# Banded attention: weights normalised inside their transposition, by diagonal tiles of reciprocals; squares of x moved to ScalarE, two merge gates computed earlier, and four changes of instruction order

## The reference, cut to what matters

```python
# start of block 1: modulated norms of x (512 tokens) and ctx (256 tokens)
h = rms_norm(x, g) * (1 + scale) + shift          # scale, shift = silu(c) @ w_mod
# each of the two layers of block 2
h = _rmsnorm(x, g_mix[l])
y_a = _mla(...)
y_b = _hgrn2(...)                                  # gates f = lb + (1-lb) * sigmoid(z), log f, scans
y_c = _window_gqa(c_q, c_k, c_v, rel_bias, c_sink[l])
merged = (jax.nn.sigmoid(gate_a) * (y_a @ w_br_a[l])
          + jax.nn.sigmoid(gate_b) * (y_b @ w_br_b[l])
          + jax.nn.sigmoid(gate_c) * (y_c @ w_br_c[l]))
x = x + merged @ w_out[l]
# _window_gqa: 8 heads of 64, blocks of 128 queries, each against 3 blocks of 128 keys
s = q @ k.T * 64 ** -0.5 + bias                    # bias: one relative-position line per head
m = maximum(max(s), sink)
p = exp(s - m)
p = p / (sum(p) + exp(sink - m))
o = p @ v
```

## Time and profile before

| | us |
|---|---|
| median of 3 runs (3956.91 to 3962.54) | 3962.54 |
| the profiled execution, its own time | 3960.44 |
| its span | 3958.6 |
| TensorE busy | 3691.1 (93%) |
| VectorE busy | 1956.9 (49%) |
| ScalarE busy | 1513.3 (38%) |
| GpSimd busy | 839.1 (21%) |
| mean granted TensorE clock | 0.959 |

### The profile page before, as it was taken

How to read it: one execution, slowest core, us unless ns; L and a number is a source line. 1 busy time by engine, 2 the same in 40 slices (tenths; PEclk the granted TensorE clock), 3 DMA queues, 4 the chain that set the end, 5 groups by cost and what they waited for, 6 DMA issues and landing times.

```text
span 3958.6 us, 60620 instructions
## 1 busy us (share of the span) xinstructions
PE 3691.1 (93%) x25506; PEld 3021.2 (76%) x25506; DVE 1956.9 (49%) x3020; ACT 1513.3 (38%) x2536; POOL 839.1 (21%) x832
## 2 busy tenths in 40 slices
PE   6989888999999989997999999998899799999998
PEld 3678877987888757786888788875677688878886
DVE  6656555535534565645333543437466533454343
ACT  4533223323323346644233422234565422343222
POOL 2222122221211123442110020202254311002120
PEclk7989998989999999998999999999999899999999
DMA  6310120013222202110223222220111022322222
GB/s 236 121 40 3 23 60 8 3 54 106 96 96 96 72 20 75 59 65 33 96 98 122 73 96 96 96 86 32 59 65 60 27 96 96 107 96 93 99 96 85
DMA packets 81111, 300.87 MB, mean 76 GB/s; under 512 B 8776, under 2 KB 9928, under 8 KB 79944
## 3 DMA queue, kind: packets, MB, share of 16 engines
q1 hardware_dynamic: 80840, 296.99, 22.0%
HBM read 292.76 MB, written 4.19 MB: 75 GB/s over the span
## 4 chain that ended last, share of the span: by engine, by line
PE 74%; DVE 11%; ACT 6%; issue 5%; POOL 3%; DMA 1%; SPq 0%; DVEq 0%; POOLq 0%; ACTq 0%
PE ps L208 72%; DVE wlo L239 2%; PE ps L213 1%; DVE he L247 1%; DMA wraw<-weights 1%; DVE ac L247 1%; ACT whi L227 1%; DVE hc L2419 1%; ACT ha L227 1%; DVE ha L239 1%; POOL p L243 1%; DVE ss L247 1%; ACT wp L228 1%; ACT L227 1%; DVE q L239 1%
## 5 line engine op out<-in xcount | busy, mean ns | idle before, releaser
L239 DVE TENSOR_TENSOR wlo<-wraw,whi 128x1024 fp32r<-128x1024 f32 x537 | 690.0, 1289 | 796.0 <-ACT whi L227 795.5
L208 PE MATMUL ps<-hh,whi 128*128 128x512 f32 x1840 | 728.7, 396 | 9.6 <-DVE hl L239 4.6
L208 PE MATMUL ps<-hl,whi 128*128 128x512 f32 x1840 | 720.5, 392 | 0.0
L208 PE MATMUL ps<-hh,wlo 128*128 128x512 f32 x1840 | 720.3, 391 | 0.0
L227 ACT ACTIVATE whi<-wraw 128x1024 fp32r<-128x1024 f32 x537 | 559.9, 1049 | 237.8 <-PE ps L208 187.1
L208 PEld LDWEIGHTS ps<-hh,whi 128*128 128x128 f32 x1840 | 347.8, 189 | 88.9 <-ACT hh L227 5.9
L208 PEld LDWEIGHTS ps<-hh,wlo 128*128 128x128 f32 x1840 | 348.0, 189 | 73.7
L208 PEld LDWEIGHTS ps<-hl,whi 128*128 128x128 f32 x1840 | 348.2, 189 | 70.5
L208 PE MATMUL ps<-u,u 64*64 64x64 f32 (+2 forms) x6016 | 229.2, 229 | 25.5 <-DVE u L239 16.8
L208 PEld LDWEIGHTS ps<-u,u 64*64 64x64 f32 (+1 forms) x6016 | 209.7, 140 | 42.8 <-DVE u L239 18.6
L208 PE MATMUL ps<-gh,whi 128*128 128x512 f32 x528 | 205.4, 389 | 0.0
(11 more groups left out here) (399 smaller groups left out, 7056.2 us busy)
## 6 DMA issues: line engine op xcount, KB each, us to landing
wraw<-weights SPq DMA_DIRECT2D x537, 512.0 KB, 3.2
x<-xT SPq DMA_DIRECT2D x2, 2048.0 KB, 9.8
bias_lines<-ln SPq DMA_DIRECT2D x1, 2048.0 KB
xmf<-memT SPq DMA_DIRECT2D x2, 1024.0 KB, 4.6
out<-x SPq DMA_DIRECT2D x1, 2048.0 KB, 6.2
bias<-bias_lines SPq DMA_DIRECT2D x1, 1536.0 KB, 8.7
con<-consts SPq DMA_DIRECT2D x1, 1379.0 KB, 16.6
ctxt<-ctxT SPq DMA_DIRECT2D x1, 1024.0 KB, 18.5
```

What stands on the lines that cost most here:

```text
L208: self.last, self.open = self.e.matmul(out, lhsT, rhs, start=start, stop=stop, skip_group_check=skip), True
L239: return self.e.tensor_tensor(out, a, b, op)
```

## The change

Seven edits, of which the first two belong to `window`.

1. VectorE makes only the reciprocals (`dve_inverse`). GpSimd writes, for each of the four row blocks, a 128x128 tile `dg` with the reciprocals on its diagonal, and TensorE turns the weights by an ordinary product with that tile, in place of a transposition by the identity. The multiplications of the weights on both engines go.
2. The gate projections of merge step 0 for the branches b and c are made in `window`: b ahead of the scores of step 1, c ahead of the turns of step 4. Gate b is copied to `stash`, later to `pre`, and its sigmoid stays in `merge`; gate c holds its PSUM bank.
3. All squares of x and ctx are made on ScalarE; GpSimd adds them in pairs (4 additions in place of 7), and TensorE sums four tiles in place of one: 16 products for x in place of 4, 8 for ctx in place of 2.
4. In the start, VectorE and ScalarE feed fewer weight blocks ahead before their next own step.
5. In `chunks` of half 0, VectorE feeds one block more before the bias add `dve_mod`.
6. The DMA of `bias_lines` is issued by ScalarE, not SP.
7. In `hgrn`, head 0, ScalarE takes the logarithms ahead of the values.

```diff
+            L.stash = self.sb("pre", W + 19968, [128, 512])
+            L.dg = self.ring(f"dg{l}", [self.sb("dg", W + 17920 + 128 * i, [128, 128]) for i in range(4)], lambda l=l: K.ended("hgrn", l))
+            L.pre = self.sb("pre", W + 33280, [128, 512])
...
+    def pool_pairs(self, tag, sq):
+        pool = self.pool
+        for k in range(0, 8, 2):
+            pool.wait_ge(self.act.at("sq", *tag, k + 1))
+            pool.tt(sq[k], sq[k], sq[k + 1], ALU.add).then_inc(pool("sq2", *tag, k // 2), 1)
...
-        K.pe_sums(lat, [K.HSQ[:, 0, :]], 4, lambda k: K.pool.at("acc", *lat))
+        K.pe_sums(lat, [K.HSQ[:, k, :] for k in range(0, 8, 2)], 4, lambda k: K.pool.at("sq2", *lat, k))
...
-        K.act_squares(lat, [K.HSQ[:, k, :] for k in ks8], [K.x[:, k, :] for k in ks8], K.loaded("x"))
+        K.act_all_squares(lat, [K.HSQ[:, k, :] for k in ks8], [K.x[:, k, :] for k in ks8], K.loaded("x"))
...
-        K.act_feed("mod", 1, ahead=2)
+        K.act_feed("mod", 1, ahead=0)
...
-        K.dve_feed("mod", 1, ahead=1)
+        K.dve_feed("mod", 1, ahead=0)
         K.dve_mod(0)
...
+            if (hg, kind, i, step) == (1, "q", 1, 0):
+                act.wait_ge(act.at("ln"))
+                act.e.dma_start(K.line, K.LN.unsqueeze(1).broadcast_to([8, 128, 512])).then_inc(K.s_load["lines"], 16)
...
-                K.dve_feed("c", *z)
                 new, old = K.mod_step(hg, c)
+                K.dve_feed("c", *z, ahead=1 if new is None else 2)
...
+    def dve_inverse(self, tag, n):
+        dve, act, sm = self.dve, self.act, self.sml[tag]
+        su, re = sm[:, 16:16 + n], sm[:, 24:24 + n]
+        dve.wait_ge(act.at("sink", *tag), act.at("p", *tag, n - 1))
+        dve.tt(su, su, re, ALU.add).then_inc(dve("su", *tag), 1)
+        dve.wait_ge(dve.at("su", *tag))
+        dve.e.reciprocal(re, su).then_inc(dve("re", *tag), 1)
+        dve.also("sml", *tag)
...
+                for dd in range(2):
+                    lns(i, dd)
                 if i == 0:
                     values()
-                for dd in range(2):
-                    lns(i, dd)
...
+            if c == 1:
+                K.pe_gate(l, 0, "b")
...
+            if c == 4:
+                K.pe_gate(l, 0, "c", hold=True)
...
-                        pe.wait_ge(K.divided(z, n))
+                        pe.wait_ge(K.pool.at("dg", *z, n), act.at("p", *z, n))
                         for j in range(k1 - k0):
-                            pe.tr(b[:, j * 128:j * 128 + 128], L.wP[z][:, n, j * 128:j * 128 + 128], K.con("id"))
+                            pe.mm(b[:, j * 128:j * 128 + 128], L.wP[z][:, n, j * 128:j * 128 + 128], L.dg[(*z, n)])
...
+                if (c, e) == (0, 1):
+                    act.wait_ge(pe.at("mg", l, 0, "b"), K.ended("hgrn", l))
+                    act.cp(L.stash, ps["mg", l, 0, "b"]).then_inc(act("stash", l), 1)
+                    act.also("ps", "mg", l, 0, "b")
...
+            if c == 2:
+                K.dve_feed("mg", l, 0, "b")
+            if c == 3:
+                K.dve_feed("mg", l, 0, "b", ahead=2)
...
-            K.pool_divide(z, [p[:, n, 0:w] for n, _, _, w, _ in K.spans()])
+            for n in range(4):
+                d = L.dg.take(pool, *z, n)
+                pool.wait_ge(K.dve.at("re", *z))
+                pool.tt(d, K.con("id"), K.sml[z][:, 24 + n:25 + n].broadcast_to([128, 128]), ALU.mult).then_inc(pool("dg", *z, n), 1)
...
+    def pe_gate(self, l, j, n, hold=False):
+        K = self
+        K.proj(("mg", l, j, n), K.win(l, "g" + n, j), [(K.ps.take(K.pe, "mg", l, j, n, hold=hold), K.h["mix", l])])
...
+                early = j == 0 and n == "b"
+                act.wait_ge(act.at("pre", l) if early else K.pe.at("mg", l, j, n))
+                act.a(g, L.pre if early else ps["mg", l, j, n], ACT.Sigmoid).then_inc(act("mg", l, j, n), 1)
...
-            if b == K.block_of["c", 1, "q", 1] + NRAW:
-                K.load("lines", K.line, K.LN.unsqueeze(1).broadcast_to([8, 128, 512]), act.at("ln"))
```

More of the change, by code:

```diff
@@ L735, in squared, with act_all_squares @@
         return (self.dve if k % 2 else self.act).at("sq", *tag, k)
+    def act_all_squares(self, tag, sq, xs, *ready):
+        act = self.act
+        for k in ks8:
+            act.wait_ge(*ready)
+            act.a(sq[k], xs[k], ACT.Square).then_inc(act("sq", *tag, k), 1)
+    def pool_pairs(self, tag, sq):
[3 more added lines that the diff above has]
+            pool.tt(sq[k], sq[k], sq[k + 1], ALU.add).then_inc(pool("sq2", *tag, k // 2), 1)
     def pe_sums(self, tag, sq, nt, ready):
@@ L894, in pe_start @@
         K.pe_mod(0, range(4, 8))
-        K.pe_sums(ctx, [K.CSQ[:, 0, :]], 2, lambda k: K.pool.at("acc", *ctx))
+        K.pe_sums(ctx, [K.CSQ[:, k, :] for k in range(0, 8, 2)], 2, lambda k: K.pool.at("sq2", *ctx, k))
         K.pe_mod(1, range(4))
@@ L912, in act_start @@
         K.act_feed("mod", 2)
-        K.act_squares(lat, [K.HSQ[:, k, :] for k in ks8], [K.x[:, k, :] for k in ks8], K.loaded("x"))
+        K.act_all_squares(lat, [K.HSQ[:, k, :] for k in ks8], [K.x[:, k, :] for k in ks8], K.loaded("x"))
         K.act_mod(2, K.mrow)
-        K.act_squares(ctx, [K.CSQ[:, k, :] for k in ks8], [K.CT[:, k, :] for k in ks8], K.loaded("ctx"))
+        K.act_all_squares(ctx, [K.CSQ[:, k, :] for k in ks8], [K.CT[:, k, :] for k in ks8], K.loaded("ctx"))
         K.act_mod(3, K.mrow)
         K.act_mod(0, K.mrow)
-        K.act_feed("mod", 1, ahead=2)
+        K.act_feed("mod", 1, ahead=0)
         K.act_shift(lat, range(4), K.x, K.HHI, 0)
@@ L940, in dve_start @@
         lat, ctx = ("lat",), ("ctx",)
-        K.dve_feed("mod", 2)
-        K.dve_squares(lat, [K.HSQ[:, k, :] for k in ks8], [K.x[:, k, :] for k in ks8], K.loaded("x"))
         K.dve_feed("mod", 2, ahead=2)
-        K.dve_squares(ctx, [K.CSQ[:, k, :] for k in ks8], [K.CT[:, k, :] for k in ks8], K.loaded("ctx"))
-        K.dve_feed("mod", 3, ahead=1)
+        K.dve_feed("mod", 3, ahead=0)
         K.dve_mod(2)
@@ L948, in dve_start @@
         K.dve_root(lat, 4, 1.0 / 1024)
-        K.dve_feed("mod", 0, ahead=1)
+        K.dve_feed("mod", 0, ahead=0)
         K.dve_mod(3)
@@ L970, in dve_scale @@
         for k in ks8:
-            dve.wait_ge(K.pe.at("rb", *tag), dve.at("gain", which), K.squared(tag, k))
+            dve.wait_ge(K.pe.at("rb", *tag), dve.at("gain", which), K.act.at("sq", *tag, k))
             dve.stt(v[:, k, :], v[:, k, :], K.gain[:, which, k:k + 1], ALU.mult, b[:, 0:T], ALU.mult).then_inc(dve("nv", *tag, k), 1)
@@ L985, in pool_start @@
         for tag, sq, nt in ((("lat",), K.HSQ, 4), (("ctx",), K.CSQ, 2)):
-            for k in range(1, 8):
-                pool.wait_ge(K.squared(tag, k - 1), K.squared(tag, k), pool.at("acc0", *tag, k - 1) if k > 1 else None)
-                pool.tt(sq[:, 0, :], sq[:, 0, :], sq[:, k, :], ALU.add).then_inc(pool("acc0", *tag, k), 1)
-            pool.also("acc", *tag)
-            if tag == ("lat",):
-                pool.wait_ge(K.loaded("consts"))
+            K.pool_pairs(tag, [sq[:, k, :] for k in ks8])
+            pool.wait_ge(K.loaded("consts"))
             K.pool_root(tag, nt)
@@ L2666, in act_window @@
         for c in range(5):
+            if c == 1:
+                K.act_feed("mg", l, 0, "b")
+            if c == 4:
+                act.wait_ge(act.at("stash", l), act.at("exped", l))
+                act.cp(L.pre, L.stash).then_inc(act("pre", l), 1)
+            if c == 3:
+                K.act_feed("mg", l, 0, "b", ahead=2)
             for i in (2 * c - 2, 2 * c - 1) if c > 0 else ():
@@ L2711, in dve_window @@
                     z = ("ws", l, 2 * c - 2 + e)
-                    K.dve_divide(z, [L.wP[z][:, n, 0:w] for n, _, _, w, _ in K.spans()], sink=True)
+                    K.dve_inverse(z, 4)
             for e in range(2) if c < 4 else ():
@@ L2796, in pe_merge @@
             for n in "abc":
-                bg, bb = ps.take(pe, "mg", l, j, n), ps.take(pe, "mb", l, j, n)
-                K.proj(("mg", l, j, n), K.win(l, "g" + n, j), [(bg, h)])
+                if j > 0 or n == "a":
+                    K.pe_gate(l, j, n)
+                bb = ps.take(pe, "mb", l, j, n)
                 cols = slice(j * 128, j * 128 + 128)
@@ L2817, in act_merge @@
                 g = L.mg.take(act, l, j, n)
-                act.wait_ge(K.pe.at("mg", l, j, n))
-                act.a(g, ps["mg", l, j, n], ACT.Sigmoid).then_inc(act("mg", l, j, n), 1)
-                act.also("ps", "mg", l, j, n)
+                early = j == 0 and n == "b"
+                act.wait_ge(act.at("pre", l) if early else K.pe.at("mg", l, j, n))
+                act.a(g, L.pre if early else ps["mg", l, j, n], ACT.Sigmoid).then_inc(act("mg", l, j, n), 1)
+                if not early:
+                    act.also("ps", "mg", l, j, n)
                 K.act_feed("mb", l, j, n)
```

8 lines of the change are left out of this document (6 added, 2 removed).

## The result

The changed kernel takes 3934.14 us (3931.06 to 3938.89, 4 runs) where the kernel before takes 3962.54: a ratio of 0.9932, 95% interval 0.9915 to 0.9949. The profiled execution has a span of 3929.9 us. The forecast was 3935. The sum came out, but not all of its terms: the lines, the logarithms and the early gates bring the time, the start and the chunks are worth nothing that these runs can tell, and the tiles cost time, which stayed hidden as long as they were counted together with the gates. The experiments show it.

What follows compares the result with a forecast made beforehand. TensorE, holding 74% of the chain of waits, was taken as the bound. Gates and tiles -8.8, lines -9.5, logarithms -5.6, start -2 and chunks -1 sum to -26.9 us, forecast 3935, range 3917 to 3952.

Steps and rivals of the forecast that it cites:

- Merge, -10.9 a layer: Merge: two gates of 5.4 us each leave it, where nothing else hides them, -10.9 us a layer.
- Window, +6.5 a layer: Window: steps 2 and 3 cost +3.2 us each, step 1 +0.4, step 4 -0.4; +6.5 us a layer.
- the term -8.8 for both layers: Window and merge: early gates and diagonal tiles as one term, 6.5 - 10.9 = -4.4 us a layer.
- That the tiles pay: Turns in the window: tiles counted with the early gates in one term of -8.8 us for both layers.
- The lines, -9.5: DMA of the lines: from ScalarE's queue, TensorE's 7.29 us wait and 2.2 us of half speed go, -9.5 us.
- Logarithms, -2.8 a layer: hgrn, first head: logarithms during the values' projection take 2.8 us a layer off TensorE's 6.9 us of waits.
- The start, -2: Start: shorter waits for ctx and mrow against added products on TensorE, -2 us, between -6.6 and +4.5.
- The chunks' block ahead, -1: Chunks of half 0: VectorE's one block more ahead of eight bias adds, -1 us, from 0 to -10.
- A: Window: rival that the clock stays at full, steps 2 and 3 cost nothing, sum -40, 3922.5 us; chance 0.18.
- B: DMA of the lines: rival that they hold up the weights all the same, 3945 to 3958 us; chance 0.14.
- C: Window: rival that the clock stays at half throughout, +16 us a layer, 3976 us, slower than before; chance 0.04.
- D: Lines and window: rival that the stall stays and the window costs the merge's gain, -8.6, 3954 us; chance 0.07.

Runs made afterwards that it cites:

- e7: The changed kernel with the root of ctx ahead of the scaling of x on VectorE: 3929.81 us, ratio 0.9913.
- e9: The changed kernel measured once more, unchanged: 3941.3 us, ratio 0.9935 to the kernel before.
- e10: The changed kernel with the start of before (squares and additions on their old engines, old blocks ahead): 3932.03 us, ratio 0.9921.
- e6: The changed kernel without the tiles, multiplications and transpositions as before, gates still early: 3932.75 us, ratio 0.9912.
- e5: The kernel before with the diagonal tiles only, the gates staying in the merge: 3972.51 us, ratio 1.0019.
- e2: The kernel before with only the logarithms of head 0 moved ahead of the values in hgrn: 3953.0 us, ratio 0.9976.
- e1: The kernel before with only the DMA of the lines issued by ScalarE: 3953.56 us against 3963.6.

## Why the forecast came out, step by step

- **Merge, -10.9 a layer.** Right: -13.3 us at the merge's first product of layer 0, -24.2 behind it, 10.9 us for two gates.
- **Window, +6.5 a layer.** +3.45 in layer 0 and +6.6 in layer 1 in this trace. In layer 0 the loop was right, and one size in it was wrong, the length of the turns. A tile at 0.4 us: 0.399. The turns at ych + 4.6: + 4.4 and + 4.8. The turns of steps 2 and 3 at 7.9 us: 6.34 and 6.33, since the clock was full again 3.4 us after they began (half until 1796.0 and 1813.1), not 7. From ych to ych these steps take 16.7 and 17.1 us in place of 18.4, and that is the whole difference of 6.5 and 3.45. In layer 1 the clock fell at the turns of step 1, too, which take 6.33 us in place of 4.70: up to the first ych 2.3 us are added and not 0.4, in steps 2 and 3 2.0 each and not 3.2. There 6.6 agrees with 6.5 because two errors cancel. In e7, e9 and e10 the clock fell at the turns of step 1 in both layers (6.33 us each time), so the -7.4 of the changed kernel's layer 0 is the lucky one. Over four traces with tiles and gates the term -8.8 for both layers measures -9.5 to -11.7.
- **That the tiles pay.** The prediction took gates and tiles as one term and never priced the tiles alone. By the traces they cost some 5 us for both layers beside the gates (e6) and 9 alone (e5), and the gates alone bring 18 to 28 in time. The prices of a turn were right (0.23 against 0.12 us), and so was it that GpSimd's last multiplication is on the path and goes: some 0.9 us of TensorE's waits within the turns of a step go with it. What was missing is the comparison. By the prediction's own loop, keeping the transpositions adds only the weight block, 1.2 us in two steps, 2.4 in place of 6.5 a layer.
- **The lines, -9.5.** The mechanism was right, the size wrong for the edit: -13.3 in seven traces at the lines' own place. The missing part is the 2.45 us wait at 530 and 3.4 us of half clock behind it, from 535.1 to 538.5, which are worth up to 1.7 us; with 7.29 + 2.2 that makes 13.6. In the changed kernel's own trace only 10.2 are left at that place, since another 6.8 us of half clock stand from 499 to 505.8. That no block was late held.
- **Logarithms, -2.8 a layer.** -2.8 of waits to the digit, and half a microsecond besides: -3.3 in e2.
- **The start, -2.** Failed, though 62 was forecast and 61.43 seen: over 13 traces it is -0.7, within their scatter, and alone it is slower by 0.03 to 0.26%. The sum came sooner (45.1 in place of 48.4) but the prediction overlooked VectorE's scaling of x between sum and root. It was in the trace of before as well, 5.34 us from 46.87 on; there TensorE still had weight products to do beside it.
- **The chunks' block ahead, -1.** Nothing is seen of it. From the first projection to block 60, where its eight bias adds stand, the six kernels with it take 0.7 to 1.4 us more than before, and the seven others without it 0.8 to 1.5.
- **Rivals.** A: the clock fell in steps 2 and 3 as before, though for less long. The Trainium skill's page TensorE: Matmul & The Clock Gate (Part 4: PE-mode transpose) has it that a transposition doesn't count as busy in the same way. In steps 2 and 3, from the idle stretch on, the half clock never lasted over 6.8 us in the six traces with tiles, and 10.2 or 13.7 us at least once in each of the eight with transpositions, which fits. It doesn't prove it, for the products also keep TensorE busy for longer. What it gives back is less than the products cost. B fell with e1, C with the clocks of 0.83 in steps 2 and 3, D with e1 and with window and merge, which give 11.7 us in this trace.

That the median came within 1 us of the forecast is partly luck. The profiled execution gained 28.7 us where 26.9 were forecast: window and merge 11.7 for 8.8, the lines' column 13.3 for 9.5, the logarithms 5.1 for 5.6, start and chunks 2.0 for 3, and then 3.4 us were lost in half 0, in the rest and behind the last block, in code that no edit touches. The forecast has no term for that. The ratios of the five parts alone add up to -0.78%, the changed kernel has -0.65 to -0.68%.

## What to carry to other kernels

Move dense work that nothing depends on into the waits of a latency-bound loop, and put the preparation it needs into the idle time of the other engines, not ahead of the instruction that the loop waits for. Give a large, late-needed transfer its own queue when weight blocks stream through the first. Before an edit is bundled with another into one term, price it alone: here the gates carried the tiles.
